# The q·k products and the transposes of q, moved from a unit's end into the next unit's merge stage, with a PSUM bank of their own

## The chip, the cores and the metric

The kernel runs on one core of a Trainium2 chip. Its engines are TensorE (PE in the profile, PEld its weight loads), VectorE (DVE), ScalarE (ACT), GpSimd (POOL) and the queue of SyncE (SP), from which all DMAs go. The metric is the device time in microseconds of one execution: 1201.17 us, the median of 3 runs (1200.78 to 1202.61).

## The reference

One layer of a gated DeltaNet block over 1024 tokens of width 1024, 8 heads (key width 128, value width 256), and a final RMSNorm. All is float32.

```python
h = rms_norm(x, norm_w) * (1 + scale) + shift                 # adaLN: scale, shift, gate from silu(c) @ ada_w
qkv, z, b, a = split(h @ w_in)
q, k, v = silu(causal_short_conv(qkv, conv_w))                # 4 taps
q = l2_norm(q) * DK ** -0.5;  k = l2_norm(k)
beta = sigmoid(b);  g = -exp(a_log) * softplus(a + dt_bias);  gc = cumsum(g)      # in a chunk
decay = exp(gc_i - gc_j), j <= i
T = inverse(I + strict_lower(beta * k k^T * decay))
attn = (q k^T) * decay
# chunks in order, S the state (128 x 256):
v_new = T (beta v - beta exp(gc) k S)
o = exp(gc) q S + attn v_new
S = exp(gc_last) S + (exp(gc_last - gc) k)^T v_new
y = (rms_norm(o, gdn_norm_w) * silu(z)) @ w_out
out = rms_norm(x + gate * y, final_norm_w)
```

## The kernel before, in words

A head is handled in two **units** of 512 tokens, so there are 16 units, u = 0 to 15; a unit is four chunks of 128 tokens. The engines run programs of their own, each written out by hand, and meet at semaphores (`passed(eng, name, u, n)` waits until the named step of unit u is done n times). On each engine the order of the work is the order of the code: unit 0, then a loop whose body holds an odd unit and an even one, then unit 15.

While unit u's recurrence runs, the projections `h @ w_in` for unit u+1 are woven in as filling: `project` (L406) makes six tiles of 24 matmuls of 512 columns, three for each of the 8 parts of the contraction (`h_hi,w_hi`, `h_lo,w_hi`, `h_hi,w_lo`). How many matmuls go where is in the table FILLS. For a tile, ScalarE writes `w_hi` (`split_hi`, L685), GpSimd then writes `w_lo` (`split_lo`, L1344, four instructions), and TensorE waits for it in front of the tile. In even units GpSimd and ScalarE also gate and split the head's output weights (L1358, L1351, L691).

A unit has these stages, with the TensorE lines:

- **Merge stage.** The inverse of the triangular matrix is put together from blocks of 16 in three levels; each has products `merge_p` (L466, bank 5), which VectorE masks (`merge_p_out`, L1041), and `merge_d` (L475, L482, L478, bank 4), which VectorE subtracts (`merge_d_out`, L1049, L1051, L1055). `merge_p` of level 0 waits for `t_done`, which `spread_t` (L1028) of VectorE gives. Between these stand the fills; after level 1 `turn_k` (L415) and `decay_exponents` (L421) for the next unit, then `k_gram` (L428) and `turn_v` (L454).
- **Chunk stage.** For each chunk products with the state (L538, L542), with the inverse (L550), and two with the new values (L560, L563); `turn_o` (L491) transposes the output, VectorE gates it (`gate_o`, L954), ScalarE and GpSimd split it into `og_hi` (L745) and `og_lo` (L1394), and `out_project` (L506) multiplies it by the output weights into banks 6 and 7. VectorE adds these to y (`add_y`, L963). `out_project` of a chunk waits for `og_lo` of that chunk and for `add_y` of the chunk before it, as both use the same two banks.
- **End.** `turn_o` of chunk 3, `out_project` of chunk 2, then for the next unit `qk` (L435: four 128x128 products of k and q into bank 2) and `turn_q` (L442: four transposes of q into bank 5), then `out_project` of chunk 3.

VectorE ends a unit with the convolution of the next unit's v (L927, L930, `pre` copies L934 to L940), `gate_o` of chunk 3, `add_y` of chunk 2, `attn` (L1021: bank 2 times decay into `attn_t`), `spread_t`, and `add_y` of chunk 3. In the merge stage it begins with `merge_p_out`, `eps_of_q` (L1068, which waits for the sums of squares of q), `silu` (L947) and the convolution of the last v tile.

ScalarE begins a unit with `square` of q (L725: four Squares of the transposed q, each with a sum), then `evacuate` (L697) and `split_hi` of weight tile 1, then the tanh (L711) of the last v tile, which waits for that tile's convolution on VectorE, then `evacuate` and `split_hi` of weight tile 2. In unit 0 there is only the wait for `gate_done` between the Squares and the tanh.

Of the kernel before, what the change touches and what calls it, by code (L numbers as in the profile page):

```python
# [10 lines left out]
P = 128  # L11
# [28 lines left out]
def build(nc, x, c, ada_w, ada_b, norm_w, w_in, conv_w, a_log, dt_bias, gdn_norm_w, w_out,  # L40
          final_norm_w, out):
    ctx = ExitStack()
    with ctx:
# [20 lines left out]
        ident = sb("ident", [P, P])  # L64
# [16 lines left out]
        q_ss = sb("q_ss", [P, NCH])  # L81
# [17 lines left out]
        cvq = part(1024, 1024, to="p (s t) -> p s t", s=2)  # L99
# [111 lines left out]
        def passed(eng, name, u, n):  # L211
            value = at(name, u, n)
            if not isinstance(value, int) or value > 0:
                eng.wait_ge(S[name], value)
# [178 lines left out]
        def _(pe):  # L393
# [37 lines left out]
            def qk(u, par):  # L431
                passed(pe, "silu_done", u - 1, Q_POS + 1)
                passed(pe, "r_done", u - 1, 4)
                for c in range(NCH):
                    mm = nc.tensor.matmul(bank[2][:, c * P:(c + 1) * P], cvk[:, par, c * P:(c + 1) * P],  # L435
                                          cvq[:, par, c * P:(c + 1) * P], start=True, stop=True)
                mm.then_inc(S["qk_done"], 1)

            def turn_q(u, par):
                passed(pe, "o_done", u - 1, 4)  # L440
                for c in range(NCH):
                    mm = nc.tensor.transpose(bank[5][:, c * P:(c + 1) * P], cvq[:, par, c * P:(c + 1) * P], ident[:, :])  # L442
                mm.then_inc(S["q_turned"], 1)

            def turn_v(u):
                passed(pe, "silu_done", u - 1, V_POS + 2)
                passed(pe, "attn_done", u, 1)
                passed(pe, "og_done", u - 1, 4)
                if isinstance(u, int) and u == 0:
                    pe.wait_ge(gate_done, 2)  # L450
                for c in range(NCH):
                    for m in range(2):
                        o = (c % 2) * DV + m * P
                        mm = nc.tensor.transpose(bank[2 + c // 2][:, o:o + P], cvv[:, m, c * P:(c + 1) * P],  # L454
                                                 ident[:, :])
                mm.then_inc(S["v_turned"], 1)

            def merge_p(u, lv):
                if lv == 0:
                    passed(pe, "t_done", u, 1)  # L460
                    passed(pe, "q_squared", u, 4)
                else:
                    passed(pe, "merge_d_out", u, lv)
                p_bank = halves(bank[5], lv, (lv % 2) * DV)
                for c in range(NCH):
                    mm = nc.tensor.matmul(p_bank[:, c, :, :], nmat[:, c, :], pairs(tm, lv)[:, c, :, 0, :],  # L466
                                          start=True, stop=True)
                mm.then_inc(S["merge_p"], 1)
# [42 lines left out]
            def body(hd, par, last=False, begun=0, fills=FILLS):  # L511
                u = 2 * hd + par
# [3 lines left out]
                def fill(n):  # L516
                    n = min(n, 2 * MM - pos[0]) if last else n
                    project(u, par, pos[0], pos[0] + n, last)
                    pos[0] += n

                for lv in range(3):
                    merge_p(u, lv)
                    fill(in_merge[lv][0])
                    merge_d(u, lv)
                    fill(in_merge[lv][1])
                    if lv == 1 and not last:
                        turn_k(u + 1, 1 - par)
                        decay_exponents(u + 1)
# [38 lines left out]
                turn_o(u, NCH - 1)  # L567
                for n in range(2):
                    out_project(u, NCH - 2, n, hd, par, not last)
                if not last:  # L570
                    qk(u + 1, 1 - par)
                    turn_q(u + 1, 1 - par)
                for n in range(2):
                    out_project(u, NCH - 1, n, hd, par, not last)

# [82 lines left out]
            project(-1, 1, 104, 110)  # L658
            k_gram(0, 0)
            project(-1, 1, 110, 144)  # L660
            qk(0, 0)
            turn_q(0, 0)
            project(0, 0, 0, MM)
            pe.wait_ge(gate_summed, KT)
            passed(pe, "attn_done", 0, 1)
            for n in range(2):
                mm = nc.tensor.matmul(bank[2 + n][:, :], ones[:, :], gate_bc[:, n * 512:(n + 1) * 512],
                                      start=True, stop=True)
# [9 lines left out]
        def _(act):  # L678
# [96 lines left out]

            def body(hd, par, last=False, first=False):
                u, other = 2 * hd + par, 1 - par
                square(u, "q", bank[5], q_ss)
                if first:
                    act.wait_ge(gate_done, 2)  # L780
                else:
                    evacuate(u - 1, 5)
                    split_hi(u, hd, par, 1)
                tanh(u - 1, 5, 3, cvv[:, 1, :])
                if last:
                    evacuate_z(u, 0, 0)
# [121 lines left out]
        def _(dve):  # L908
# [162 lines left out]
            def body(hd, par, last=False, first=False):  # L1071
                u, other, nxt = 2 * hd + par, 1 - par, hd + par
                merge_p_out(u, 0)
                eps_of_q(u)
                if not first:
                    silu(u - 1, 4, cvv[:, 0, :])
# [68 lines left out]
                gate_o(u, 3)  # L1145
                add_y(u, par, 2)
                if not last:
                    attn(u + 1)
                    spread_t(u + 1)
                else:  # L1150
                    norm_y(3)
                    norm_y(4)
                    norm_y(5)
                    norm_y(6)
# [113 lines left out]
                sum_gate(k)  # L1268
            dve.wait_ge(gate_summed, KT)
            decay_k(0, 0)  # L1270
            attn(0)
            conv(-1, 1, 0, 2)
            invert_blocks(0, 0, BLK - 1)
            silu(-1, 4, cvv[:, 0, :])
# [206 lines left out]
```

## Time and profile before

| | us |
|---|---|
| median of 3 runs | 1201.17 (1200.78 to 1202.61) |
| the profiled execution's own time | 1203.63 |
| its span | 1201.8 |
| TensorE busy | 1114.4 (93%) |
| weight loads busy | 920.6 (77%) |
| VectorE busy | 836.7 (70%) |
| GpSimd busy | 599.9 (50%) |
| ScalarE busy | 448.1 (37%) |

The mean granted clock of TensorE over the profiled span was 0.97 of full speed; its two levels are 2.4 GHz (1.00) and 1.2 GHz (0.50). The timeline gives for each row the start, the length from the start of the first instruction to the end of the last (a matmul is shown longer than the distance to the next one, since they overlap), and in brackets the engine's idle time ahead of it with what ended it. Unit 0 begins at about 110 us, unit 5 ends and unit 6 begins at about 520 us, and an odd and an even unit together take 136.5 us.

### The profile page before, as it was taken

To read this page: it belongs to the slowest core of one execution; us is meant where nothing else is said; L and a number is where in the kernel's file an instruction comes from. 1 tells how busy PE (TensorE), PEld (TensorE's weight loads), DVE (VectorE), ACT (ScalarE), POOL (GpSimd) and SP (SyncE) were. 2 spreads that over 40 slices of the span, in tenths; PEclk is the share of its full clock that TensorE was granted. 3 is DMA by queue.
4 is the path that set the end of the run, shared out by engine and by line. 5 is a ranking of instruction groups with operands and counts; after the bars stand their busy time and mean duration, and the time that the engine had idled before them with its cause. 6 is when DMAs were issued, how large, how long until landed. Compare 5 with 4: busy or idle time off the path is not lost.

```text
span 1201.8 us, 19507 instructions
## 1 busy us (share of the span) xinstructions
PE 1114.4 (93%) x5628; PEld 920.6 (77%) x5628; DVE 836.7 (70%) x1888; ACT 448.1 (37%) x1038; POOL 599.9 (50%) x819
## 2 busy tenths in 40 slices
PE   3896899999999999999999999999999999999984
PEld 2665688887888788887888788887888788887863
DVE  4776586776858586775858586685868677685835
ACT  4642333333242433433333333334243333334333
POOL 2353544565444744466345754456444853456413
PEclk9897899999999999999999999999999999999988
DMA  9922222213122321223221221223221222213103
GB/s 311 326 58 60 63 58 62 55 57 81 40 62 57 80 57 44 56 60 76 55 62 40 81 65 43 62 55 81 57 59 43 79 56 55 62 40 97 33 25 123
DMA packets 150754, 88.31 MB, mean 73 GB/s; under 512 B 29446, under 2 KB 145320, under 8 KB 150696
## 3 DMA queue, kind: packets, MB, share of 16 engines
q1 hardware_dynamic: 150696, 87.73, 26.6%
q14 instruction: 45, 0.37, 0.1%
q8 instruction: 13, 0.21, 0.1%
HBM read 78.28 MB, written 9.44 MB: 73 GB/s over the span
## 4 chain that ended last, share of the span: by engine, by line
PE 64%; POOL 12%; DVE 11%; issue 7%; ACT 2%; DMA 1%; SPq 0%; DVEq 0%; POOLq 0%; ACTq 0%
PE bank L406 31%; PE bank L506 11%; POOL w_lo L1344 5%; POOL wo_lo L1351 4%; DVE y L963 3%; DVE work L930 3%; PE bank L550 2%; PE bank L466 2%; PE bank L560 2%; PE bank L538 2%; PE bank L542 2%; PE bank L482 2%; PE bank L475 2%; PE bank L563 2%; PE bank L588 1%
## 5 line engine op out<-in xcount | busy, mean ns | idle before, releaser
L1344 POOL TENSOR_TENSOR w_lo<-w_raw,w_hi 128x256 fp32r<-128x256 f32 x384 | 333.5, 898 | 254.9 <-ACT w_hi L685 254.8
L406 PE MATMUL bank<-h_hi,w_hi 128*128 128x512 f32 x760 | 320.2, 421 | 20.8 <-POOL w_lo L1344 20.8
L406 PE MATMUL bank<-h_lo,w_hi 128*128 128x512 f32 x760 | 313.4, 412 | 0.0
L406 PE MATMUL bank<-h_hi,w_lo 128*128 128x512 f32 x760 | 310.6, 409 | 0.0
L406 PEld LDWEIGHTS bank<-h_hi,w_hi 128*128 128x128 f32 x760 | 146.5, 193 | 53.7 <-POOL w_lo L1344 24.8
L930 DVE SCALAR_TENSOR_TENSOR work<-pre,cw,work 128x512 f32<-128x512 f32 x192 | 168.5, 878 | 14.1 <-DVE work L927 5.4
L406 PEld LDWEIGHTS bank<-h_hi,w_lo 128*128 128x128 f32 x760 | 145.6, 192 | 30.8 <-issue 0.2
L406 PEld LDWEIGHTS bank<-h_lo,w_hi 128*128 128x128 f32 x760 | 146.9, 193 | 27.8 <-issue 0.2
L1394 POOL TENSOR_TENSOR og_lo<-work,og_hi 128x256 fp32r<-128x256 f32 x64 | 47.1, 737 | 217.4 <-ACT og_hi L745 217.4
L711 ACT ACTIVATE work<-work 128x512 f32<-128x512 f32 x64 | 40.2, 628 | 271.8 <-DVE pre L940 131.0
L506 PE MATMUL bank<-wo_hi,og_hi 128*128 128x512 f32 x256 | 113.7, 444 | 10.1 <-DVE y L963 10.1
L963 DVE SCALAR_TENSOR_TENSOR y<-bank,o_rs,y 128x512 f32<-128x512 f32 x128 | 89.5, 739 | 23.4 <-PE bank L506 23.4
L1007 DVE TENSOR_TENSOR work<-work 32x15 f32<-32x15 f32 (+7 forms) x240 | 70.1, 292 | 47.0 <-DMA work<-n_dram 39.2
L685 ACT ACTIVATE w_hi<-w_raw 128x1024 fp32r<-128x1024 f32 x96 | 101.2, 1054 | 1.6 <-DMA w_raw<-in_gdn_w_in 1.6
L506 PE MATMUL bank<-wo_hi,og_lo 128*128 128x512 f32 x256 | 100.7, 393 | 0.0
L506 PE MATMUL bank<-wo_lo,og_hi 128*128 128x512 f32 x256 | 100.3, 392 | 0.0
L947 DVE SCALAR_TENSOR_TENSOR work<-work 128x512 f32<-128x512 f32 x96 | 76.7, 799 | 3.2 <-ACT work L711 1.4
L756 ACT ACTIVATE work<-bank,k_tab 128x256 f32<-128x256 f32 x64 | 30.4, 475 | 116.4 <-PE bank L550 116.4
L954 DVE SCALAR_TENSOR_TENSOR work<-bank,small,work 128x128 f32<-128x128 f32 x128 | 38.7, 342 | 50.1 <-PE bank L491 50.1
L745 ACT ACTIVATE og_hi<-work 128x256 fp32r<-128x256 f32 x64 | 26.7, 417 | 115.6 <-DVE work L954 112.6
L506 PEld LDWEIGHTS bank<-wo_hi,og_hi 128*128 128x128 f32 x256 | 48.0, 188 | 24.1 <-POOL og_lo L1394 14.2
L1011 DVE TENSOR_TENSOR work<-work 32x15 f32<-32x15 f32 (+7 forms) x240 | 60.1, 250 | 8.3
(176 smaller groups left out, 1870.0 us busy)
## 6 DMA issues: line engine op xcount, KB each, us to landing
w_raw<-in_gdn_w_in SPq DMA_DIRECT2D x96, 512.0 KB, 4.0
work<-in_ada_w SPq DMA_DIRECT2D x8, 1024.0 KB, 9.7
w_raw<-in_gdn_w_out SPq DMA_DIRECT2D x16, 512.0 KB, 3.3
y<-in_x SPq DMA_DIRECT2D x8, 512.0 KB, 9.1
work<-in_ada_w SPq DMA_DIRECT2D x8, 512.0 KB, 6.1
n_dram<-work SPq DMA_DIRECT2D x16, 256.0 KB, 3.4
out<-y SPq DMA_DIRECT2D x8, 512.0 KB, 2.7
t_dram<-work SPq DMA_DIRECT2D x16, 64.0 KB, 1.6
```

The costliest lines, as they stand in the source:

```text
L406: mm = nc.tensor.matmul(bank[m % 2][:, :], w[:, m % 2, k, :], h[:, k, half, :], start=(r == 0), stop=(r == MM - 1))
L506: mm = nc.tensor.matmul(bank[6 + n][:, :], a[:, m, :], w[:, m, n * 512:(n + 1) * 512], start=(m == 0 and q == 0), stop=(m == 1 and q == 2))
L685: nc.scalar.activation(w_hi[:, k % 2, :, :], w_raw_k[:, k % 2, :, :], ACT.Copy).then_inc(S["w_hi_done"], 1)
L711: nc.scalar.activation(th[:, m % 2, :], cv, ACT.Tanh, scale=0.5).then_inc(S["tanh_done"], 1)
L930: o = stt(out=cv, in0=pre[:, r, j:j + HALF], scalar=tap, in1=cv, op0=ALU.mult, op1=ALU.add)
L947: stt(out=t, in0=th[:, m % 2, :], scalar=1.0, in1=t, op0=ALU.add, op1=ALU.mult).then_inc(S["silu_done"], 1)
L963: i = stt(out=yt, in0=bank[6 + n][:, :], scalar=o_rs[:, c:c + 1], in1=yt, op0=ALU.mult, op1=ALU.add)
L1007: nc.vector.tensor_tensor(tmp, blk_n[:, j:j + 1, j + 1:].rearrange("p o n -> p n o").to_broadcast(shape), blk_y[:, j:j + 1, 0:j + 1].to_br ...
L1011: nc.vector.tensor_tensor(below, below, tmp, ALU.subtract).then_inc(S["base_step"], 1)
L1344: i = nc.gpsimd.tensor_tensor(w_lo[:, k % 2, j:j + 2, :], w_raw_k[:, k % 2, j:j + 2, :], w_hi[:, k % 2, j:j + 2, :].bitcast(F32), ALU.subt ...
L1351: o = nc.gpsimd.tensor_tensor(wo_lo[:, i, j:j + 256], w_raw[:, 1 - i, j:j + 256], wo_hi[:, i, j:j + 256].bitcast(F32), ALU.subtract)
L1394: nc.gpsimd.tensor_tensor(og_lo[:, :, :], og, og_hi[:, :, :].bitcast(F32), ALU.subtract).then_inc(S["og_lo_done"], 1)
```

## The change

The products and transposes for unit u no longer stand at the end of unit u-1 but in unit u, behind `merge_p` of level 0. The transposes write bank 3 in place of bank 5, so `merge_p` no longer waits for the Squares of q, and `turn_v`, which overwrites banks 2 and 3, now does. On ScalarE the Squares move behind `evacuate` and `split_hi` of weight tile 1 (in unit 0 behind the wait for `gate_done`). On VectorE `attn` moves from the end of unit u-1 to the place between `merge_p_out` and `eps_of_q` of unit u. No instruction is added or dropped.

```diff
--- before.py
+++ after.py
@@ -431,23 +431,23 @@
             def qk(u, par):
                 passed(pe, "silu_done", u - 1, Q_POS + 1)
                 passed(pe, "r_done", u - 1, 4)
+                if isinstance(u, int) and u == 0:
+                    pe.wait_ge(gate_done, 2)
                 for c in range(NCH):
                     mm = nc.tensor.matmul(bank[2][:, c * P:(c + 1) * P], cvk[:, par, c * P:(c + 1) * P],
                                           cvq[:, par, c * P:(c + 1) * P], start=True, stop=True)
                 mm.then_inc(S["qk_done"], 1)
 
             def turn_q(u, par):
-                passed(pe, "o_done", u - 1, 4)
+                passed(pe, "og_done", u - 1, 4)
                 for c in range(NCH):
-                    mm = nc.tensor.transpose(bank[5][:, c * P:(c + 1) * P], cvq[:, par, c * P:(c + 1) * P], ident[:, :])
+                    mm = nc.tensor.transpose(bank[3][:, c * P:(c + 1) * P], cvq[:, par, c * P:(c + 1) * P], ident[:, :])
                 mm.then_inc(S["q_turned"], 1)
 
             def turn_v(u):
                 passed(pe, "silu_done", u - 1, V_POS + 2)
                 passed(pe, "attn_done", u, 1)
-                passed(pe, "og_done", u - 1, 4)
-                if isinstance(u, int) and u == 0:
-                    pe.wait_ge(gate_done, 2)
+                passed(pe, "q_squared", u, 4)
                 for c in range(NCH):
                     for m in range(2):
                         o = (c % 2) * DV + m * P
@@ -458,7 +458,7 @@
             def merge_p(u, lv):
                 if lv == 0:
                     passed(pe, "t_done", u, 1)
-                    passed(pe, "q_squared", u, 4)
+                    passed(pe, "o_done", u - 1, 4)
                 else:
                     passed(pe, "merge_d_out", u, lv)
                 p_bank = halves(bank[5], lv, (lv % 2) * DV)
@@ -520,6 +520,9 @@
 
                 for lv in range(3):
                     merge_p(u, lv)
+                    if lv == 0:
+                        qk(u, par)
+                        turn_q(u, par)
                     fill(in_merge[lv][0])
                     merge_d(u, lv)
                     fill(in_merge[lv][1])
@@ -567,9 +570,6 @@
                 turn_o(u, NCH - 1)
                 for n in range(2):
                     out_project(u, NCH - 2, n, hd, par, not last)
-                if not last:
-                    qk(u + 1, 1 - par)
-                    turn_q(u + 1, 1 - par)
                 for n in range(2):
                     out_project(u, NCH - 1, n, hd, par, not last)
 
@@ -658,11 +658,8 @@
             project(-1, 1, 104, 110)
             k_gram(0, 0)
             project(-1, 1, 110, 144)
-            qk(0, 0)
-            turn_q(0, 0)
             project(0, 0, 0, MM)
             pe.wait_ge(gate_summed, KT)
-            passed(pe, "attn_done", 0, 1)
             for n in range(2):
                 mm = nc.tensor.matmul(bank[2 + n][:, :], ones[:, :], gate_bc[:, n * 512:(n + 1) * 512],
                                       start=True, stop=True)
@@ -775,12 +772,12 @@
 
             def body(hd, par, last=False, first=False):
                 u, other = 2 * hd + par, 1 - par
-                square(u, "q", bank[5], q_ss)
                 if first:
                     act.wait_ge(gate_done, 2)
                 else:
                     evacuate(u - 1, 5)
                     split_hi(u, hd, par, 1)
+                square(u, "q", bank[3], q_ss)
                 tanh(u - 1, 5, 3, cvv[:, 1, :])
                 if last:
                     evacuate_z(u, 0, 0)
@@ -1071,6 +1068,7 @@
             def body(hd, par, last=False, first=False):
                 u, other, nxt = 2 * hd + par, 1 - par, hd + par
                 merge_p_out(u, 0)
+                attn(u)
                 eps_of_q(u)
                 if not first:
                     silu(u - 1, 4, cvv[:, 0, :])
@@ -1145,7 +1143,6 @@
                 gate_o(u, 3)
                 add_y(u, par, 2)
                 if not last:
-                    attn(u + 1)
                     spread_t(u + 1)
                 else:
                     norm_y(3)
@@ -1268,7 +1265,6 @@
                 sum_gate(k)
             dve.wait_ge(gate_summed, KT)
             decay_k(0, 0)
-            attn(0)
             conv(-1, 1, 0, 2)
             invert_blocks(0, 0, BLK - 1)
             silu(-1, 4, cvv[:, 0, :])
```

TensorE where unit 5 ends and unit 6 begins (L506 is `out_project`, L435 `qk`, L442 `turn_q`, L466 `merge_p`, L406 the fill; L214 are register and wait instructions), before:

```order
L506 MATMUL bank<-wo_lo,og_hi 128x512
L506 MATMUL bank<-wo_hi,og_lo 128x512
L435 MATMUL bank<-work 128x128 x4
L442 MATMUL bank<-ident,work 128x128 x4
L506 MATMUL bank<-wo_hi,og_hi 128x512
...
L506 MATMUL bank<-wo_hi,og_lo 128x512
L214 ISA x2
L466 MATMUL bank<-work 128x64 x4
L214 ISA
L214 REGISTER_ALU
L406 MATMUL bank<-h_hi,w_hi 128x512
```

And now (L437 is `qk`, L444 `turn_q`):

```order
L506 MATMUL bank<-wo_hi,og_lo 128x512
L214 ISA x2
L466 MATMUL bank<-work 128x64 x4
L214 ISA
L437 MATMUL bank<-work 128x128 x4
L444 MATMUL bank<-ident,work 128x128 x4
L214 ISA
L214 REGISTER_ALU
L406 MATMUL bank<-h_hi,w_hi 128x512
```

The eight instructions have left the place between the `out_project` of chunk 2 and that of chunk 3 and stand behind `merge_p`, ahead of the first fill.

ScalarE at the same place (L745 the last `og_hi` of unit 5, L725 the Squares, L697 `evacuate`, L685 `split_hi`, L711 the tanh), before:

```order
L745 ACTIVATE og_hi<-work 128x256
L214 ISA
L214 REGISTER_ALU x3
L725 ACTIVATE work,q_ss<-bank 128x128
...
L725 ACTIVATE work,q_ss<-bank 128x128
L214 ISA x2
L697 ACTIVATE pre<-bank 128x512
L214 REGISTER_ALU
L685 ACTIVATE w_hi<-w_raw 128x1024
L214 REGISTER_ALU x2
L711 ACTIVATE work<-work 128x512
```

And now (L742 `og_hi`, L694 `evacuate`, L682 `split_hi`, L722 the Squares, L708 the tanh):

```order
L742 ACTIVATE og_hi<-work 128x256
L214 ISA x2
L694 ACTIVATE pre<-bank 128x512
L214 ISA
L682 ACTIVATE w_hi<-w_raw 128x1024
L214 REGISTER_ALU x3
L722 ACTIVATE work,q_ss<-bank 128x128
...
L722 ACTIVATE work,q_ss<-bank 128x128
L214 REGISTER_ALU x2
L708 ACTIVATE work<-work 128x512
```

The Squares have moved behind the first `split_hi` of the unit, and still stand ahead of the tanh and of the second `split_hi`.

## Rows read from the trace of the kernel before

**Rows 1.** Waits of TensorE: us in total, times, longest us.
```profile
PE bank L406 <- POOL w_lo L1344: 20.8, 10, 2.3
PE bank L506 <- DVE y L963: 10.1, 18, 1.6
```

**Rows 2.** Timeline of TensorE, end of unit 5 and start of unit 6.
```profile
514.81 0.40 PE L506 MATMUL bank<-wo_hi,og_lo 128*128 128x512 f32 x1
515.04 1.06 PE L435 MATMUL bank<-work 128*128 128x128 f32 x8
515.93 0.60 PE L442 MATMUL bank<-ident,work 128*128 128x128 f32 x4
517.19 0.47 PE L506 MATMUL bank<-wo_hi,og_hi 128*128 128x512 f32 x1 [0.66 <-DVE y L963]
...
520.01 1.00 PE L466 MATMUL bank<-work 128*128 128x64 f32 x8
```

**Rows 3.** Timeline of VectorE and GpSimd, end of unit 5.
```profile
500.73 0.61 DVE L954 SCALAR_TENSOR_TENSOR work<-bank,small,work 128x128 f32<-128x128 f32 x2 [1.80 <-PE bank L491]
...
515.12 0.61 DVE L954 SCALAR_TENSOR_TENSOR work<-bank,small,work 128x128 f32<-128x128 f32 x2
515.64 1.40 DVE L963 SCALAR_TENSOR_TENSOR y<-bank,o_rs,y 128x512 f32<-128x512 f32 x2
...
516.96 0.68 DVE L1021 TENSOR_TENSOR work<-bank,work 128x512 f32<-128x512 f32 x1
...
516.26 0.72 POOL L1394 TENSOR_TENSOR og_lo<-work,og_hi 128x256 fp32r<-128x256 f32 x1 [4.75 <-ACT og_hi L745]
```

**Rows 4.** Timeline of ScalarE, start of unit 6.
```profile
516.80 0.28 ACT L725 ACTIVATE work<-bank 128x128 f32<-128x128 f32 x1 [0.62 <-PE bank L442]
...
518.27 0.59 ACT L697 ACTIVATE pre<-bank 128x512 f32<-128x512 f32 x1
...
528.98 0.63 ACT L711 ACTIVATE work<-work 128x512 f32<-128x512 f32 x1 [9.16 <-DVE pre L938]
```

**Rows 5.** Timeline of VectorE, start of unit 6.
```profile
521.87 0.16 DVE L1068 TENSOR_SCALAR q_eps<-q_ss 128x4 f32<-128x4 f32 x1
...
525.62 0.42 DVE L1049 TENSOR_TENSOR work<-work,bank 128x256 f32<-128x256 f32 x1 [0.68 <-PE bank L482]
```

**Rows 6.** Timeline of GpSimd, weight tile 2 of unit 6.
```profile
531.20 4.25 POOL L1344 TENSOR_TENSOR w_lo<-w_raw,w_hi 128x256 fp32r<-128x256 f32 x4 [1.05 <-ACT w_hi L685]
```

**Rows 7.** TensorE's wait in unit 6; stretch 550 to 554 (columns: stretch, us, busy, PEclk, DMA).
```profile
550.46 0.80 PE L406 MATMUL bank<-h_hi,w_hi 128*128 128x512 f32 x1 [2.29 <-POOL w_lo L1344]
...
550.00:554.00 4.00, 3.54 (x9) 2.84 (x10) 0.00 (x0) 0.00 (x0) 0.41 (x1) 0.57 0.56 150
```

**Rows 8.** Timeline of the start of unit 0.
```profile
110.43 1.97 PE L466 MATMUL bank<-work 128*128 128x64 f32 x8 [7.49 <-DVE work L1028]
114.16 0.79 PE L406 MATMUL bank<-h_hi,w_hi 128*128 128x512 f32 x1 [1.76 <-POOL w_lo L1344]
...
109.21 0.63 ACT L711 ACTIVATE work<-work 128x512 f32<-128x512 f32 x1 [10.42 <-DVE gate_bc L1279]
...
111.35 2.76 POOL L1344 TENSOR_TENSOR w_lo<-w_raw,w_hi 128x256 fp32r<-128x256 f32 x4 [14.77 <-ACT w_hi L685]
```

**Rows 9.** Two short waits of TensorE in unit 0, and stretches behind each.
```profile
137.25 0.67 PE L538 MATMUL bank<-state,work 128*128 128x256 f32 x2 [1.75 <-ACT work L739]
140.38 0.53 PE L406 MATMUL bank<-h_hi,w_hi 128*128 128x512 f32 x1 [2.03 <-POOL w_lo L1344]
...
137.30:138.30 1.00, 1.00 (x4) 0.59 (x4) 0.35 (x1) 0.00 (x0) 1.00 (x2) 1.00 0.04 7
140.80:144.00 3.20, 3.20 (x9) 2.52 (x8) 0.00 (x0) 0.00 (x0) 0.00 (x0) 0.50 0.46 98
```

**Rows 10.** Timeline, end of unit 4 (TensorE) and start of unit 5 (VectorE).
```profile
450.82 0.47 PE L506 MATMUL bank<-wo_hi,og_hi 128*128 128x512 f32 x1 [0.31 <-DVE y L963]
...
456.90 0.42 DVE L1041 TENSOR_TENSOR pm<-bank,pair_mask 128x256 f32<-128x256 f32 x1 [1.63 <-issue]
```

## The prediction, made before the changed kernel was run

> **What bounds the kernel now.** I read the busy shares first: TensorE is busy for 93% of the span, and the other engines for 70% or less. So the next view is that of TensorE's waits. There are few: it waits 10 times for `w_lo` and 18 times, briefly, for VectorE's y in front of `out_project` [rows 1]. Next I read the timeline of one boundary between units on all engines, because that is where the change cuts, then the place in the even units where TensorE waits for `w_lo`, then the start of unit 0.
>
> At the boundary the reader is to see three things. First, the moved instructions take 1.49 us of TensorE (515.04 to 515.93 + 0.60 = 516.53), and TensorE then still waits 0.66 us, until 517.19 [rows 2]. Second, what ends that wait does not depend on them: VectorE has been busy without a gap since 500.73, when a transpose of TensorE's released it; it reaches `gate_o` of chunk 3 at 515.12 and `add_y` of chunk 2 at 515.64, which ends at 517.04, and GpSimd's `og_lo` ends at 516.98 [rows 3]. Third, the first work behind `merge_p` at 520.01 is filling that runs without a gap [rows 2]. So the 1.49 us stand today in a wait that is there anyway, and are moved to a place where TensorE has no wait.
>
> **The change part by part.**
>
> *TensorE, end of a unit.* With the eight instructions gone TensorE reaches `out_project` of chunk 3 at 514.81 + 0.40 = 515.21 and waits until 517.19, so 1.98 us in place of 0.66 [rows 2]. At the end of an even unit the wait is 0.31 now [rows 10]; with about 1.3 more it becomes 1.6. Gain: nothing, as the start at 517.19 is VectorE's. That VectorE no longer does `attn` (0.68 us, [rows 3]) does not help, since it stood behind `add_y` of chunk 2. It makes `spread_t` 0.6 us earlier, and TensorE comes to `merge_p` only at 520.01, without a wait, so that is worth nothing either.
>
> *TensorE, merge stage.* 1.49 us are put in behind `merge_p`. What follows is filling and `merge_d`, and the next wait of TensorE in an odd unit is that at its end, behind VectorE's last uninterrupted stretch, which begins at a transpose of TensorE's [rows 3]. The insertion therefore moves that too, and the price is the full 1.49 us in each of the 8 odd units: 11.9 us. In odd units VectorE has a gap of 1.63 us ahead of `merge_p_out` [rows 10], behind which the Squares of q are nearly done (about 1.0 us more, and 1.3 us later `merge_d` is what VectorE waits for), so VectorE adds nothing there. That odd units then have no second cost is a choice: between 0 and 0.6 us each (the length of `attn`) I take 0.
>
> *ScalarE and VectorE, even units.* The Squares now wait for transposes that end at about 520.01 + 0.9 + 1.49 = 522.4. Today they start 0.27 us after the transposes' end and take 1.47 us (516.80 to 518.27, [rows 4]), so they end at 524.1, and `eps_of_q`, which VectorE runs in order, moves from 521.87 to 524.2, by 2.3 us. Of this 0.68 us go into the gap ahead of `merge_d_out` [rows 5]; 1.65 us stay on the convolution of v, on the tanh of ScalarE that waits for it (528.98) [rows 4], and on `split_hi` and `split_lo` of weight tile 2 (531.20), for which GpSimd already waits 1.05 us now [rows 6]. From there GpSimd works nearly without a gap through the output weights to tile 3, for which TensorE waits 2.29 us [rows 7]. So both ends of that wait move, TensorE's arrival by 1.49 and GpSimd's end by 1.65, and each of the 7 even units from u = 2 on costs 1.65 us: 11.6 us. `evacuate` and `split_hi` of tile 1 start about 2.0 us earlier (516.2 in place of 518.27, [rows 4]), and with them `split_lo` of tile 1 and the DMA of the output weights behind it; but GpSimd then waits at tile 2, so the 2 us are spent waiting. With GpSimd and VectorE disturbing each other at other places I keep 1.2 to 2.3 us as the bounds of this term.
>
> *Unit 0.* Before, q was squared long ahead of the tanh at 109.21. Now ScalarE waits for `turn_q`, which stands behind `merge_p` of unit 0, and the tanh, `evacuate` and `split_hi` of the weight tile that TensorE needs next stand behind the Squares. `merge_p` starts 0.68 us earlier (VectorE has no `attn` ahead of `spread_t`), at 109.75. It takes 1.97 us there, twice the 1.00 us of [rows 2], as the granted clock is low; so the moved 1.49 us take about 2.8, to 114.5. Squares: 0.27 + 1.47, to 116.3. From tanh to GpSimd's start is 111.35 - 109.21 = 2.14, to 118.4; from there to TensorE's fill 114.16 - 111.35 = 2.81, to 121.2, against 114.16 [rows 8]. That is 7.0 us late. The later waits of unit 0 are all behind VectorE or GpSimd work that follows from these merges, so none of it comes back. Bounds: 5 (some comes back at the waits for k and `w_lo`) and 9 (the longer gap keeps the clock low for longer).
>
> *Clock.* A drop costs about 1.7 us: over 550 to 554 the granted clock is 0.57, so that it was at 1.2 GHz for 0.86 of 4 us, in which half the work is lost [rows 7]. It follows the wait for `w_lo` in each of the 7 even units. The new wait of 1.98 us at the end of the 8 odd units lies between a gap of 1.75 us, after which the clock was granted in full, and one of 2.03 us, after which it was 0.50 [rows 9]. If all 8 fall it costs 13.6 us; against that some of the 7 drops that are there now may go, up to 11.9 us. I take 0 net as the middle and keep both ends. On this the Trainium skill, "TensorE: Matmul & The Clock Gate", section "Why this matters for your kernels", warns only of gaps above about 3 us between bursts of matmuls. By that rule the new gaps are free and the sum is unchanged; the trace disagrees with it, as the clock fell behind 2.03 us of idle time, and so the worse end stays in the range.
>
> *Sum.* 7.0 + 11.9 + 11.6 = 30.5 us. On the profiled execution's own 1203.63 us that gives 1234.1; the median of the runs is 2.5 us below that execution, so the prediction is 1232 us. Unit 15 is counted among the odd ones; it has less filling, and its waits behind the merge stage all follow from merges, so it takes the 1.49 us in full. The other moves (`turn_v` waiting for the Squares, which by the times above are done long before it; the wait for `gate_done` in front of `qk`, fulfilled when the tanh at 109.21 starts) cost nothing.
>
> **The rivals.**
>
> *The clock falls at the odd units' ends too.* The mechanism above with 6 to 8 drops of 1.7 us and none lost at `w_lo`: 1232 + 10 to 13.6, about 1244. For it: a gap of 2.03 us sufficed once. Against: one of 1.75 us did not, and 1.98 lies between.
>
> *The wait for `w_lo` swallows the insertion.* If VectorE's delay does not reach the tanh, or GpSimd's time is made up, the end of GpSimd's chain stays, TensorE comes 1.49 us later to a wait of 2.2 us, and the even units cost nothing: 1201.2 + 7.0 + 11.9 = 1220. For it: the early `split_lo` of tile 1. Against: GpSimd's wait of 1.05 us at tile 2, which ScalarE ends [rows 6].
>
> *The other side: the early weight split shortens the wait for `w_lo`.* If what limits GpSimd in even units were its start on tile 1 (2.0 us earlier now) and not ScalarE's tile 2, the wait of about 2.2 us and its drop of 1.7 would go in 7 units, 27.3 us, against 15 x 1.49 = 22.4 put in, with unit 0 then also unharmed: 1201.2 - 27.3 + 22.4 = 1196. It decides at GpSimd's start on tile 2: it must come before 531.2 and not after. Against it is again that GpSimd waits there.
>
> *The change does nothing on the path.* If VectorE reached `gate_o` earlier by what it is spared, the end of the unit would give back 1.49 us each time, leaving unit 0 alone: about 1208, or 1201 if unit 0 hides it as well. Against: `attn` stands behind the wait's end [rows 3].
>
> **How the numbers follow.** Forecast 0.66 (its own range 1222 to 1241), clock rival 0.14, swallowed in even units 0.10, the other side 0.04, nothing on the path 0.06. The time is the forecast's, 1232. The range goes down to 1219, which takes in the swallowing, and up to 1246. A change within 0.2% cannot be told from none here. Faster 0.04; same 0.03 (half of the last case); slower 0.93.
>
> **What would show it right or wrong.** In the changed profile TensorE's wait in front of L506 at the end of units should be near 2.0 us after odd and 1.6 us after even ones, some 30 us in all in place of 10.1; VectorE's `eps_of_q` should wait for ScalarE in even units by over 1 us; the wait for `w_lo` should still be about 2.2 us in even units; an odd and an even unit together should take about 139.7 us in place of 136.5; and in unit 0 TensorE's fill behind `merge_p` should start near 121 us. The prediction is wrong if the pair stays at 136.5 us, if the wait for `w_lo` shrinks to nothing, or if unit 0 starts its fill near 114 us.

## The result, and the profile after

The changed kernel takes 1230.08 us (median of 4 runs, 1227.61 to 1232.38) against 1200.97 us for the kernel before, measured beside it: 29.1 us more, ratio 1.0236 (95% interval 1.0221 to 1.0252). The forecast was 1232, with 1219 to 1246 as its range.

Its profiled execution took 1229.18 us, with a span of 1227.4 in place of 1201.8. TensorE is busy for 1112.3 us, as before (1114.4); it has the same work and waits more. Its waits (columns as in [rows 1]):

```profile
PE bank L506 <- DVE y L960: 30.1, 18, 2.0
PE bank L406 <- POOL w_lo L1340: 23.1, 11, 6.5
...
PE bank L541 <- DVE state L1122: 6.8, 7, 1.4
```

The wait in front of `out_project` at the ends of units has grown from 10.1 to 30.1 us, and the wait for the state (L541 is L538 of before), which was 1.6 us in 2 places, is now 6.8 us in 7. The timeline of TensorE at the end of unit 7 and the start of unit 8, and the end of unit 8, answers to [rows 2] and [rows 10]:

```profile
670.80 0.47 PE L506 MATMUL bank<-wo_hi,og_hi 128*128 128x512 f32 x1 [1.97 <-DVE y L960]
673.63 1.00 PE L466 MATMUL bank<-work 128*128 128x64 f32 x8
...
675.41 0.60 PE L444 MATMUL bank<-ident,work 128*128 128x128 f32 x4
675.77 0.47 PE L406 MATMUL bank<-h_hi,w_hi 128*128 128x512 f32 x1
...
741.69 0.47 PE L506 MATMUL bank<-wo_hi,og_hi 128*128 128x512 f32 x1 [1.63 <-DVE y L960]
```

The gap of 0.66 us is now 1.97, that of 0.31 is 1.63. The first fill starts 2.14 us behind the start of `merge_p`; before it was 0.81 behind it (657.36 against 656.55 in the same unit), so what was put in is 1.33 us.

The other engines in the same unit, answering to [rows 4 to 7]:

```profile
677.81 0.17 DVE L1065 TENSOR_SCALAR q_eps<-q_ss 128x4 f32<-128x4 f32 x1 [1.40 <-ACT work L722]
681.12 0.41 DVE L1046 TENSOR_TENSOR work<-work,bank 128x256 f32<-128x256 f32 x1
...
676.21 0.28 ACT L722 ACTIVATE work<-bank 128x128 f32<-128x128 f32 x1 [5.00 <-PE bank L444]
683.73 0.63 ACT L708 ACTIVATE work<-work 128x512 f32<-128x512 f32 x1 [5.96 <-DVE pre L935]
...
685.95 4.03 POOL L1340 TENSOR_TENSOR w_lo<-w_raw,w_hi 128x256 fp32r<-128x256 f32 x4 [4.15 <-ACT w_hi L682]
704.84 0.53 PE L406 MATMUL bank<-h_hi,w_hi 128*128 128x512 f32 x1 [2.12 <-POOL w_lo L1340]
```

VectorE waits 1.40 us for the Squares in front of `q_eps`, and the gap ahead of `merge_d_out` (L1046) is gone. GpSimd waits 4.15 us for weight tile 2 where it waited 1.05: its earlier start on tile 1 was spent waiting. It starts on that tile 15.15 us into the unit (685.95 less 670.80), against 14.01 in [rows 6] (531.20 less 517.19), so 1.1 us later and not 1.65. TensorE's wait for `w_lo` ends 34.04 us into unit 8; before it ended 33.11 us into the same unit.

Unit 0, answering to [rows 8]:

```profile
109.53 1.97 PE L466 MATMUL bank<-work 128*128 128x64 f32 x8 [7.49 <-DVE work L1025]
120.66 0.80 PE L406 MATMUL bank<-h_hi,w_hi 128*128 128x512 f32 x1 [6.50 <-POOL w_lo L1340]
```

From one start of `out_project` of chunk 3 to the next I have the lengths of the units:

| stretch | before | after | difference |
|---|---|---|---|
| start to end of unit 0 | 177.38 | 183.83 | 6.45 |
| units 1, 3, ... 13, mean (us each) | 66.34 | 67.51 | 1.17, 8.2 in 7 |
| units 2, 4, ... 14, mean (us each) | 70.24 | 71.91 | 1.67, 11.7 in 7 |
| behind that | 68.35 | 67.66 | -0.7 |

That sums to the 25.6 us between the two spans. The medians differ by 29.1, as the profiled execution of before (1203.63 us) was itself 2.7 us above its median, and that of after 0.9 below.

The even units, which before took 70.1 to 70.4 each, now take 70.89 (u = 8) to 72.63 (u = 4). What separates them is the clock (columns as in the second row of [rows 7]; the stretches lie behind the ends of units 1, 3, 5, 9 and 11):

```profile
253.00:255.00 2.00, 2.00 (x6) 1.60 (x5) 0.00 (x0) 0.00 (x0) 2.00 (x3) 0.50 0.00 0
393.00:395.00 2.00, 2.00 (x6) 1.54 (x6) 0.00 (x0) 0.00 (x0) 2.00 (x4) 0.50 0.00 0
533.00:535.00 2.00, 2.00 (x6) 1.54 (x6) 0.00 (x0) 0.00 (x0) 2.00 (x4) 0.50 0.00 0
810.00:812.00 2.00, 2.00 (x10) 1.66 (x9) 0.25 (x1) 0.00 (x0) 2.00 (x3) 1.00 0.00 0
949.50:952.00 2.50, 2.50 (x7) 1.98 (x6) 0.00 (x0) 0.00 (x0) 2.50 (x4) 0.50 0.00 0
```

In this execution the clock fell to 1.2 GHz behind the gap at the ends of units 1, 3, 5, 11 and 13, and behind the wait for `w_lo` in u = 4 and 10 only. So the even units have 7 falls, as before, in other places. (All counts of falls are of one profiled execution; this one had a mean granted clock of 0.973, the other three of this kernel 0.975 to 0.977.) The four even units that begin with a fall and have none later (2, 6, 12, 14) take 72.2 on average; unit 8, with none, 70.89; unit 10, with one behind `w_lo`, 71.07. By this a fall at the start of a unit costs 1.3 us and one behind `w_lo` some 0.2; the second number rests on one pair of units. Compared in the same way inside each of the runs below that has even units of both kinds, the first is 1.1 to 1.7 us and the second 0.2 to 0.6.

### The profile page after: what moved, and what is told of

Read it like the earlier page. It is cut to its first block, busy times and chain, and to the rows that moved or that the text cites. A ratio compares the mean times of both kernels' runs of the same rounds, so it can differ in the third digit from the quotient of the medians.

```text
span 1227.4 us, 19561 instructions
## 1 busy us (share of the span) xinstructions
PE 1112.3 (91%) x5628; PEld 918.0 (75%) x5628; DVE 833.9 (68%) x1888; ACT 448.2 (37%) x1038; POOL 598.3 (49%) x819
## 4 chain that ended last, share of the span: by engine, by line
PE 59%; DVE 13%; POOL 10%; issue 9%; DMA 4%; ACT 3%; SPq 1%; DVEq 1%; ACTq 0%; POOLq 0%
PE bank L406 26%; PE bank L506 11%; POOL wo_lo L1347 4%; POOL w_lo L1340 3%; DVE work L927 3%; DVE y L960 2%; PE bank L466 2%; DMA n_dram<-work 2%; PE bank L553 2%; PE bank L541 2%; PE bank L563 2%; PE bank L545 2%; PE bank L566 1%; PE bank L588 1%; POOL w_raw L1354 1%
## 5 line engine op out<-in xcount | busy, mean ns | idle before, releaser
L406 PE MATMUL bank<-h_hi,w_hi 128*128 128x512 f32 x760 | 316.7, 417 | 23.1 <-POOL w_lo L1340 23.1
L406 PE MATMUL bank<-h_lo,w_hi 128*128 128x512 f32 x760 | 310.2, 408 | 0.0
L406 PE MATMUL bank<-h_hi,w_lo 128*128 128x512 f32 x760 | 308.2, 405 | 0.0
L406 PEld LDWEIGHTS bank<-h_hi,w_hi 128*128 128x128 f32 x760 | 144.7, 190 | 56.1 <-POOL w_lo L1340 27.6
L927 DVE SCALAR_TENSOR_TENSOR work<-pre,cw,work 128x512 f32<-128x512 f32 x192 | 165.7, 863 | 14.0 <-DVE work L924 4.4
L406 PEld LDWEIGHTS bank<-h_hi,w_lo 128*128 128x128 f32 x760 | 144.2, 190 | 30.0 <-issue 0.2
L406 PEld LDWEIGHTS bank<-h_lo,w_hi 128*128 128x128 f32 x760 | 144.9, 191 | 27.2 <-issue 0.2
L506 PE MATMUL bank<-wo_hi,og_hi 128*128 128x512 f32 x256 | 116.0, 453 | 30.1 <-DVE y L960 30.1
L708 ACT ACTIVATE work<-work 128x512 f32<-128x512 f32 x64 | 40.1, 627 | 216.9 <-DVE pre L935 108.6
L506 PE MATMUL bank<-wo_hi,og_lo 128*128 128x512 f32 x256 | 104.0, 406 | 0.0
L506 PE MATMUL bank<-wo_lo,og_hi 128*128 128x512 f32 x256 | 103.0, 402 | 0.0
L682 ACT ACTIVATE w_hi<-w_raw 128x1024 fp32r<-128x1024 f32 x96 | 101.1, 1053 | 0.7 <-DMA w_raw<-in_gdn_w_in 0.7
L1004 DVE TENSOR_TENSOR work<-work 32x15 f32<-32x15 f32 (+7 forms) x240 | 72.3, 301 | 42.6 <-DMA work<-n_dram 36.2
L506 PEld LDWEIGHTS bank<-wo_hi,og_hi 128*128 128x128 f32 x256 | 49.3, 193 | 47.3 <-POOL og_lo L1390 36.9
L722 ACT ACTIVATE work<-bank 128x128 f32<-128x128 f32 x128 | 35.5, 277 | 130.5 <-PE bank L444 99.2
L944 DVE SCALAR_TENSOR_TENSOR work<-work 128x512 f32<-128x512 f32 x96 | 73.1, 761 | 2.8 <-ACT work L708 1.0
L1008 DVE TENSOR_TENSOR work<-work 32x15 f32<-32x15 f32 (+7 forms) x240 | 64.8, 270 | 8.2
```

Of the source, the lines that this page charges most:

```text
L406: mm = nc.tensor.matmul(bank[m % 2][:, :], w[:, m % 2, k, :], h[:, k, half, :], start=(r == 0), stop=(r == MM - 1))
L506: mm = nc.tensor.matmul(bank[6 + n][:, :], a[:, m, :], w[:, m, n * 512:(n + 1) * 512], start=(m == 0 and q == 0), stop=(m == 1 and q == 2))
L682: nc.scalar.activation(w_hi[:, k % 2, :, :], w_raw_k[:, k % 2, :, :], ACT.Copy).then_inc(S["w_hi_done"], 1)
L708: nc.scalar.activation(th[:, m % 2, :], cv, ACT.Tanh, scale=0.5).then_inc(S["tanh_done"], 1)
L927: o = stt(out=cv, in0=pre[:, r, j:j + HALF], scalar=tap, in1=cv, op0=ALU.mult, op1=ALU.add)
L944: stt(out=t, in0=th[:, m % 2, :], scalar=1.0, in1=t, op0=ALU.add, op1=ALU.mult).then_inc(S["silu_done"], 1)
```

## The experiments

Each run is timed against the kernel before, and the ratio is to that. "In place of" compares with the changed kernel's 1230.1.

**Unit 0 as before.** The start-up again makes `qk`, `turn_q`, `attn` and the Squares of unit 0 (the transposes into bank 5); the core of the edit:

```diff
+            qk(0, 0)
+            turn_q(0, 0)
             project(0, 0, 0, MM)
...
                 if first:
+                    square(u, "q", bank[5], q_ss)
                     act.wait_ge(gate_done, 2)
```

> The changed kernel, but with unit 0 arranged as before: its products of q and k, its transposes of q (into bank 5), their Squares and attn stand in the start-up again; units 1 to 15 keep the change. Theory (ScalarE's tanh and weight split of unit 0 queue behind the Squares, and TensorE starves for w_lo): the fill behind the first merge_p starts near 114 us again, and of the 6.5 us that the change had lost by the end of unit 0 all come back and stay: 1230.1 - 6.5 = 1223.6. Rival (unit 0's delay only hides waits that come later anyway, its loss is in the later units): 1229 to 1231.

Measured 1220.89 us, ratio 1.0173 (1.0157 to 1.0188): 9.2 us come back. TensorE's first fill of unit 0:

```profile
113.93 0.79 PE L406 MATMUL bank<-h_hi,w_hi 128*128 128x512 f32 x1 [1.77 <-POOL w_lo L1349]
```

Unit 0 ends at 177.14 (177.38 before, 183.83 in the changed kernel), so 6.7 us of the 9.2 are unit 0's. The rest is not unit 0's own. The two profiled spans differ by 9.8 us, of which 3.3 lie in units 1 to 14. This execution has 4 falls at ends of units and one behind `w_lo`, where the other had 5 and 2; by the prices above that makes about half of the 3.3. The other half is that the even units that begin with a fall take 71.8 us on average in place of 72.2, and why they do is open.

**`eps_of_q` later on VectorE.**

```diff
                 merge_p_out(u, 0)
                 attn(u)
-                eps_of_q(u)
...
                 merge_p_out(u, 1)
+                eps_of_q(u)
```

> The changed kernel with one VectorE step moved: eps_of_q, which waits for the Squares of q, stands behind merge_p_out of level 1 and no longer ahead of the silu and the convolution. Theory (both the 1.34 us of TensorE and VectorE's wait move the even units, and the two run side by side, so that taking one away leaves the other): VectorE's wait of 1.4 us goes, even units get 0.4 us shorter, 3 us in all: 1227. Rival A (VectorE's wait for the Squares alone sets the even units, TensorE's 1.34 us are hidden behind it): 7 x 1.65 = 11.6 us come back, 1218.5. Rival B (VectorE's wait costs nothing): 1230.

Measured 1228.08 us, ratio 1.0222 (1.0207 to 1.0238), 2 us off, where 3 were expected; as its interval overlaps that of the changed kernel the size is unclear, but the 11.6 us of rival A are excluded. VectorE no longer waits for the Squares, and now waits for TensorE's `merge_d` a little later (unit 6):

```profile
542.89 0.42 DVE L1046 TENSOR_TENSOR work<-work,bank 128x256 f32<-128x256 f32 x1 [1.52 <-PE bank L482]
...
546.87 0.16 DVE L1065 TENSOR_SCALAR q_eps<-q_ss 128x4 f32<-128x4 f32 x1
```

In its profile the even units that begin with a fall of the clock take 71.9 us on average (2, 4, 6, 8, 12, 14) in place of 72.2, and the one without, u = 10, 70.23 in place of 70.89. So VectorE's wait is worth 0.3 to 0.7 us in an even unit, not 1.65. The clock fell at 6 ends of units here and at 5 there, which takes back part of the gain.

**ScalarE's order alone, on the kernel before.**

```diff
-                square(u, "q", bank[5], q_ss)
                 if first:
+                    square(u, "q", bank[5], q_ss)
                     act.wait_ge(gate_done, 2)
                 else:
                     evacuate(u - 1, 5)
                     split_hi(u, hd, par, 1)
+                    square(u, "q", bank[5], q_ss)
```

> The kernel before with one part of the change alone: on ScalarE the Squares of q stand behind evacuate and split_hi of weight tile 1, so that tile's split starts about 1.5 us earlier. Theory (GpSimd waits for weight tile 2 in any case): no change, 1200 to 1202. Rival (GpSimd's start on tile 1 sets TensorE's wait for w_lo in the even units): the wait of 2.2 us shrinks by 1.5 us in 7 units, up to 10 us faster, and with its drops of the clock gone up to 22 us.

Measured 1198.21 us, ratio 0.9979 (0.9969 to 0.9989): a little faster, where I had said no change. GpSimd does wait at tile 2 as expected (start of unit 8, at 650.79):

```profile
664.71 3.96 POOL L1345 TENSOR_TENSOR w_lo<-w_raw,w_hi 128x256 fp32r<-128x256 f32 x4 [3.09 <-ACT w_hi L685]
```

That is 13.92 us into the unit, against 14.00 before. What is earlier is the gating of the output weights on GpSimd (7.56 against 9.52 us into the unit), which no longer runs beside VectorE's silu of the second v tile (0.68 us in place of 1.07). From there the convolution, the transposes of k and GpSimd's tile 3 are 0.4 us earlier (29.44 against 29.83). The clock also fell in 3 of the 7 even units in place of 7, and the wait for `w_lo` was still 1.95 to 2.23 us; so the rival's size did not come, only its sign. The even units with a fall take 69.8 us and those without 69.35, where before all had one and took 70.24. The wait of 0.23 us in front of `turn_k` is gone in them as well. This part of the change is therefore a gain of about 0.5 us in each even unit, and the changed kernel contains it.

**Work added at the end of the units.** In the gap between the last two `out_project` TensorE makes four spare products.

```diff
+                if not last:
+                    passed(pe, "silu_done", u, Q_POS + 1)
+                    passed(pe, "r_done", u, 4)
+                    spare_products(1 - par)
                 for n in range(2):
                     out_project(u, NCH - 1, n, hd, par, not last)
```

> The changed kernel with work added: in the gap at the end of each of the units 0 to 14, between the out_project of chunk 2 and that of chunk 3, TensorE makes the four products of k and q of the next unit once more into the free bank 2, 0.9 us each time, 13 us of TensorE's time in all; nothing reads them. Theory (at 5 of the 7 odd ends after which a full even unit follows the clock fell in the profile, and each fall cost 1.4 us; the gap of 1.98 us shrinks to 1.1): faster by about 7 us in spite of the added work, 1223, with no stretch at the lower clock behind the ends of units. Rival A (the clock plays no part there): 1230. Rival B (the gap is not free): slower by up to 13 us, 1243.

Measured 1222.13 us, ratio 1.0173 (1.0158 to 1.0189): 8 us faster than the changed kernel with 13 us more work. Its wait at the ends of units (L511 is `out_project` here) is, in the view of waits,

```profile
PE bank L511 <- DVE y L969: 16.7, 18, 1.6
```

13.4 us less than 30.1: the spare products take just that much out of the gaps (1.97 becomes 1.09 us, 1.63 becomes 0.73). No fall of the clock is left behind an end of a unit, and 4 even units have one behind `w_lo`, where 2 had. The intervals of the two ratios do not touch, so it is shown that the gap is free, and that less idle time there ended the falls: none followed the 14 gaps of 1.04 to 1.10 us at odd ends in this run and in the one that fills the gap, below. A gap near 2 us does not bring a fall each time, as the next run shows.

**Work added in the merge stage.** The same four products, made twice behind `merge_p` in units 1 to 15.

```diff
-                for c in range(NCH):
+                for c in list(range(NCH)) * (1 if isinstance(u, int) and u == 0 else 2):
```

> The changed kernel with work added in the other place: in the merge stage of units 1 to 15 the four products of q and k are made twice (the first set is overwritten), 0.9 us more each. Theory (the merge stage has no wait that hides what is put in, where the end of a unit has one): slower by the full 0.9 x 15 = 13 us, 1230 + 13 = 1243, within 3 us as the falls of the clock shift. Rival A (what is put in there is partly hidden in the even units, by the wait for w_lo or behind VectorE's wait for the Squares): 7 to 9 us slower, 1238. Rival B (hidden altogether): 1230. Beside the same products at the end of the units (1222), this gives the price of a place.

Measured 1237.71 us, ratio 1.0309 (1.0293 to 1.0325): 7.6 us in place of 13, in the number rival A's case. The units say why. Unit 1 takes 251.28 - 182.86 = 68.42 us, 0.9 more than 67.52, the full price. Even units without a fall take 71.45 to 72.06 (u = 2, 10, 12, 14) against 70.89, 0.6 to 1.2 more, and only one of the odd ends (unit 7's) is followed by a fall, against 5:

```profile
253.00:255.00 2.00, 2.00 (x15) 1.80 (x13) 0.69 (x2) 0.00 (x0) 2.00 (x4) 1.00 0.00 0
...
673.80:676.00 2.20, 2.20 (x6) 1.66 (x6) 0.00 (x0) 0.00 (x0) 2.20 (x4) 0.50 0.00 0
```

Insertion at 0.9 x 15 = 13 less 4 falls at 1.3 gives 8. (By stages the spans differ by 8.6: the 7 odd units 6.2, the 7 even ones together 0.5, unit 15 2.5, as the clock fell in its chunk stage again, unit 0 and the tail -0.7.) So the place has nearly no cover in odd units and little in even ones, and fewer falls gave back 5 us. Why they were fewer is open: nothing was changed at the ends, where the gaps are still 1.98 to 2.02 us.

**The gap filled with projection work.** The changed kernel with the two edits above (unit 0, `eps_of_q`) and 6 fill matmuls moved to the end.

```diff
-        FILLS = (((12, 12), (10, 14), (6, 2)), 16,
+        FILLS = (((12, 12), (10, 14), (3, 2)), 13,
...
+                fill(6)
                 for n in range(2):
                     out_project(u, NCH - 1, n, hd, par, not last)
```

> The changed kernel with unit 0 arranged as before, eps_of_q behind merge_p_out of level 1, and 6 of the 144 projection matmuls of each unit moved into the gap at its end: 3 come from the fill behind merge_p of level 2 (6 to 3) and 3 from the fill behind turn_v (16 to 13). Theory (the gap at the end of a unit takes any work of TensorE for nothing, up to 1.6 us): 6 x 0.23 = 1.4 us in 15 units, 20 us off 1219, 1199 or somewhat less, as TensorE also comes later to the wait for w_lo. Rival (the fills taken away were covering waits for VectorE and ScalarE, or a new wait appears behind the chunk stage's DMA): 1205 to 1215.

Measured 1204.43 us, ratio 1.0026 (1.0016 to 1.0037). Of the 20 us expected off 1219 some 15 came, and the second half of the rival did too, a new wait in the chunk stage:

```profile
PE bank L509 <- DVE y L969: 16.6, 18, 1.6
...
PE bank L406 <- POOL w_lo L1351: 14.6, 10, 2.0
PE bank L545 <- DVE state L1132: 11.1, 9, 1.5
```

The wait for `w_lo` in even units is down to 1.30 us, and none of them has a fall any more; but behind it TensorE now waits 1.46 us for VectorE's state in each even unit (L545), and the gaps at the ends are 1.04 and 0.66 us and not 0.6 and 0.2. In the changed kernel that wait stood in 5 even units already, those that TensorE went through at full clock behind `w_lo`. There VectorE's chain through the inverse's blocks, which begins when their DMA lands, meets GpSimd's next weight tile. In the changed kernel, u = 8:

```profile
708.96 0.17 DVE L1004 TENSOR_TENSOR work<-work 32x15 f32<-32x15 f32 x1 [5.03 <-DMA work<-n_dram]
709.16 0.59 DVE L1008 TENSOR_TENSOR work<-work 32x15 f32<-32x15 f32 x1
709.79 0.66 DVE L1004 TENSOR_TENSOR work<-work 32x28 f32<-32x28 f32 x1
...
708.96 2.84 POOL L1340 TENSOR_TENSOR w_lo<-w_raw,w_hi 128x256 fp32r<-128x256 f32 x4 [4.17 <-ACT w_hi L682]
712.59 0.70 PE L541 MATMUL bank<-state,work 128*128 128x256 f32 x2 [1.09 <-DVE state L1122]
```

Before, with the clock fallen, GpSimd began that tile 5.6 us behind the wait for `w_lo` in place of 4.1, and these VectorE instructions, clear of it, took 0.17 to 0.19 us each:

```profile
690.92 0.17 DVE L1007 TENSOR_TENSOR work<-work 32x15 f32<-32x15 f32 x1 [5.00 <-DMA work<-n_dram]
691.13 0.18 DVE L1011 TENSOR_TENSOR work<-work 32x15 f32<-32x15 f32 x1
691.34 0.18 DVE L1007 TENSOR_TENSOR work<-work 32x28 f32<-32x28 f32 x1
```

This accounts for the low price of a fall behind `w_lo`: the time that it takes from TensorE it largely gives back in a wait (0.7 to 1.5 us in even units without the fall, none in those with it). The same meeting is behind the gaps that stayed 0.4 us too long: in the last stretch of odd units three of these instructions take 0.63 to 0.66 us beside GpSimd's tile (unit 5, 505.35 to 507.36), where two did in the changed kernel (unit 7), and from the `gate_o` that a transpose releases to the start of `add_y` of chunk 2 VectorE takes 15.32 us in place of 14.89.

**The kernel before, improved.** ScalarE's order, and 2 fill matmuls moved to the end of each unit.

```diff
-        FILLS = (((12, 12), (10, 14), (6, 2)), 16,
+        FILLS = (((12, 12), (10, 14), (4, 2)), 16,
...
+                fill(2)
                 for n in range(2):
                     out_project(u, NCH - 1, n, hd, par, not last)
```

> The kernel before with the order of ScalarE alone changed (Squares behind evacuate and split_hi of tile 1) and 2 projection matmuls of each unit moved from the fill behind merge_p of level 2 (6 to 4) to the end of the unit, in front of the out_project of chunk 3, where TensorE still waits 0.3 and 0.65 us. Theory (that wait takes 0.46 us of work, 0.3 in even units): 0.4 x 15 = 6 us, and TensorE comes 0.46 us later to the wait for w_lo: 1198.2 - 6 = 1192, down to 1189. Rival (the even units are bound behind w_lo, by the DMA of the inverse's blocks and VectorE, so only the odd ones gain): 1195.

Measured 1196.74 us, ratio 0.9966 (0.9954 to 0.9978), the fastest of all, by less than expected. The waits at the ends went from 10.1 to 4.8 us in all; in odd units a new one of 0.35 to 0.39 us stands in front of `merge_p`, which with bank 5 still waits for the Squares, and these now come later on ScalarE:

```profile
587.02 1.10 PE L466 MATMUL bank<-work 128*128 128x64 f32 x8 [0.37 <-ACT work L727]
```

Its interval overlaps that of ScalarE's order alone, so what the two matmuls are worth by themselves is not settled. The stages speak for nearly nothing: in the two profiles the odd units 3 to 13 take 66.3 to 66.4 us on average either way, and the 7 even ones together are 1.0 us longer with the matmuls moved, so the theory of 0.4 us a unit did not come, nor the rival's gain in odd units. The shorter span comes from unit 0 (0.7 us), unit 1 (0.5) and unit 15 (0.9, in which the clock did not fall this time).

## Why the prediction was right

*TensorE, end of a unit: right.* The gaps were said to become 1.98 and 1.6 us and are 1.97 to 1.99 and 1.59 to 1.63; the sum 30 us is 30.1. The spare products at the end cost nothing. (VectorE's last stretch is not quite without a gap, as it was read: it pauses twice for 0.15 us, which changes nothing.)

*TensorE, merge stage: right, the size a little high.* The term of 1.49 us in each odd unit measured 1.17, 8.2 us in 7 units. I had taken the length from the first start to the last end; the step from `merge_p` to the first fill grew by only 1.33 us, because consecutive matmuls overlap. The other 0.16 us are gone by `merge_p` of level 1 (11.17 us into unit 7 before, 12.34 now), and from there to the unit's end the delay stays at 1.17 to 1.19: nothing covers it.

*Even units: right in the sum, wrong in its parts.* The term of 1.65 us measured 1.67, and `eps_of_q` is 2.3 us late as said (7.01 us into the unit against 4.67). But the mechanism given for the 1.65 is not what made the 1.67. VectorE's delay was to reach GpSimd's tile 3 with 1.65 us; in unit 8 GpSimd started tile 2 only 1.1 us later and TensorE's wait ended 0.93 later, and moving `eps_of_q` gave back 0.3 to 0.7 us and not 1.65. What the runs show is a sum of three parts. First, the two delays: beside the kernel before with ScalarE's order changed (69.35 without a fall), unit 8 of the changed kernel (70.89) is 1.5 us longer, of which the run with `eps_of_q` moved (70.23) gives VectorE's wait 0.7 and leaves 0.9 to the insertion; as this compares single units without a fall, it is an estimate. Second, a gain that the forecast had put at nothing: ScalarE's order takes off about 0.5 us, through the wait in front of `turn_k` (0.23 us) that is gone and through VectorE's silu, which is clear of GpSimd (0.68 us in place of 1.07). Third, the clock: 5 falls of 1.3 us over 7 units make 0.9, less what 5 falls behind `w_lo` had cost.

*The step on the clock: its middle was right in the count and wrong in the price.* I set new falls at the ends against lost ones at `w_lo`, at 1.7 us each, and took 0 net. The count is indeed 7 against 7 in the even units, 5 of them moved. But the 5 lost had cost 0.2 to 0.6 us each and the 5 new ones cost 1.3, so the net was +3.5 to 5.5 us. This error and the one in the even units cancel, by luck. The clock rival, with 6 to 8 falls at 1.7 us and none lost, asked for 10 to 13.6 us and is out by its price and by the lost ones.

*The total: nearer than its parts.* The sum was 30.5 us, and the profiled executions differ by 25.6; the terms of the odd units, of unit 15 and of unit 0 were too large. That the median, 1230.1, lies within 2 us of the forecast is for 3.5 us a matter of which executions were profiled: the forecast went from an execution 2.7 us above its median, and the one after lies 0.9 below its own.

*The rule that was weighed.* The rule of the Trainium skill ("TensorE: Matmul & The Clock Gate", "Why this matters for your kernels", gaps above about 3 us) would have had no falls at all; gaps of 1.97 to 1.99 us were followed by the lower clock 5 times of 7, so for this kernel it does not hold.

*Unit 15: wrong.* It was to take 1.49 us more and took 0.5 less (53.51 and 53.02 us), and the tail behind it 0.25 less. The insertion is in it too, but before the clock fell in its chunk stage, and now it did not (about the same stretch of work in both, columns as above, before and then after):

```profile
1158.50:1164.00 5.50, 4.93 (x12) 2.91 (x11) 1.98 (x4) 1.26 (x3) 0.00 (x0) 0.50 0.00 0
```

```profile
1186.00:1192.00 6.00, 4.48 (x17) 2.33 (x16) 2.42 (x5) 3.22 (x8) 1.46 (x4) 1.00 0.00 0
```

The granted clock is 0.50 there before and 1.00 now. Before, that fall came 0.2 us behind a wait of TensorE of 1.75 us:

```profile
1157.69 1.01 PE L538 MATMUL bank<-state,work 128*128 128x256 f32 x2 [1.75 <-ACT work L739]
```

The prediction took 1.75 us as a gap after which the clock stays up, from [rows 9]. The same trace had this other case, in a stage where TensorE has little filling (12 matmuls in 5.5 us). The wait is in unit 15 of all nine profiles, and a fall followed it in four.

*Unit 0: right.* Said 7.0 us, with the fill at 121.2; it came at 120.66, 6.5 us late, and with unit 0 restored 6.7 us came back by its end.

*The rivals.* The swallowing by the wait for `w_lo` did not happen: it was 1.46 to 2.17 us (2.2 was said), and no even unit was spared; an odd and an even unit together take 139.4 us, where 139.7 was said. The other side's mechanism, an earlier weight split, had the right sign by itself (0.2% in the run with ScalarE's order alone), but through VectorE's silu and convolution and not through GpSimd's wait at tile 2, which stayed. The case of nothing on the path is out, as each odd unit took 1.17 us more.

## What to carry to other kernels

In this kernel work that stood in a wait which another engine ends cost nothing, and moved to where TensorE had none it cost 1.17 of its 1.33 us; so before moving anything, look at what ends the wait behind it. When an instruction is moved, look along every queue in which something waits for it, in the first pass of the loop above all: here a quarter of the loss was one pass in which ScalarE's weight split queued behind the Squares. And if a sum agrees with the measured time, still compare it stage by stage, because terms of it may be wrong in opposite ways.

## What was not expected of the hardware

- Gaps of the same length were followed by the lower clock in some cases and not in others: at odd ends of 1.97 to 1.99 us in 5 of 7, and in 4, 6 and 1 of 7 in the runs with unit 0 restored, with `eps_of_q` moved and with work added in the merge stage, where they are 1.98 to 2.02. What decides it no run shows. Waits of 1.46 to 1.55 us for `w_lo` had none behind them, those of 2.12 to 2.17 us two of three; before, all 7 of 2.12 to 2.29 us had.
- An idle stretch of TensorE can be paid twice or be nearly free: a fall of the clock at a unit's start cost 1.3 us, the same fall behind `w_lo` 0.2 (0.2 to 0.6 over the runs).
- VectorE's small instructions of the inverse took 0.6 to 0.7 us in place of 0.18 while GpSimd was splitting weights, and its silu 1.07 in place of 0.68 beside GpSimd's gating.
- Thirteen microseconds of useless TensorE work in the gaps at the ends of units made the changed kernel 8 us faster.
